# A hybrid attention, recurrence and convolution encoder step: small buffers moved, the last convolution tile's copies on two queues, filler matmuls in the prologue

## The chip, the cores and the metric

The kernel runs on one core of one Trainium2 chip. The metric is device time in microseconds (us), the median of several runs. A core has five engines with a queue each: PE (TensorE, matmuls), DVE (VectorE), ACT (ScalarE), POOL (GpSimd) and SP (SyncE, which here only issues transfers). They run on their own and wait for each other by semaphores. Transfers (DMAs) can be issued from SP, ACT or POOL.

## The reference, cut to what matters

Two layers over 512 prompt frames and 32 frames of a running stream (544 in all), width 1024. Layer 0 has attention and a gated recurrence side by side, layer 1 the convolution module below; each is followed by a feed-forward part.

```python
def conv_module(xn, buf, w1, b1, w_dw, b_dw, ln_g, ln_b, w2, b2):
    u = xn @ w1 + b1
    u = u[..., :D_MODEL] * jax.nn.sigmoid(u[..., D_MODEL:])
    full = jnp.concatenate([buf.astype(u.dtype), u], axis=1)
    y = lax.conv_general_dilated(full, w_dw[:, None, :], window_strides=(1,), padding='VALID',
                                 feature_group_count=D_MODEL) + b_dw      # depthwise, 31 taps
    y = jax.nn.silu(layer_norm(y, ln_g, ln_b))
    return y @ w2 + b2, full[:, -(CONV_W - 1):]

def ffn(xn, w_up, w_down):
    return jnp.square(jax.nn.relu(xn @ w_up)) @ w_down
```

## The kernel before

Activations lie with channels on the 128 partitions, in KT = 8 tiles of 544 frames. A weight matrix is streamed in **units** of 1024 x 256 (1 MB), numbered from 0 over the whole kernel. For accuracy each operand is split into a high and a low part, and every product takes three matmuls. A unit passes through: an SP load into one of two slots of `w_raw` (line 416; the load of unit n waits on `w_lo` until unit n-2 has been split), ACT's copy into `w_h` (`split_hi`, line 608), DVE's difference into `w_l` (`split_lo`, line 1514), and then PE (lines 1017, 1040 and 1056).

`keep_clock(n, bank)` issues n bf16 matmuls of 256 columns on the constant tile `ones` into a PSUM bank that is free. Their results are read by no one.

**Prologue.** SP loads the frames as rows (`x_rows`), PE turns them (line 996), DVE and ACT copy them into `resid` (semaphores `x_copied`, one for each of four PSUM slots; DVE copies tiles 0 to 5 at line 1568, ACT tiles 6 and 7 at line 661), ACT and DVE make `x_h` and `x_l`, and `together(0, 0, ...)` multiplies unit 0 tile by tile (line 1040, 96 matmuls), each tile after its `xl_ready`. `parameters()` (lines 1077 to 1085) and unit 1 (line 1017) follow. The sums of squares of the rows go to `x_ss` and their inverse roots to `x_rs`, two tiles of 128 x 5.

**Convolution.** Units U_PW1 + m, m = 0 to 7, make the two halves of channel tile m. ACT takes the sigmoid (`gate`, line 894), DVE the product (`gated_frames`, line 1912, into `glu`; it raises `slot_free[1]`). PE does 20 or, in the last tile, 24 of the 31 taps as 32 x 32 diagonal matmuls (`taps`, line 1398); for them `glu_rot` holds `glu` rotated by 32, 64 and 96 partitions, which takes six DMAs a tile, issued by POOL (lines 579 and 580, semaphores `moved[m % 2]`, 96 a tile). DVE does the other taps (line 1936) and the stream's frames (lines 1948 to 1952) and adds PE's part (`conv_sum`, line 1961). PE's order at the end is: unit of tile 7, `taps(6)`, `add_mean(0)` to `add_mean(3)` (line 1414), `taps(7)`, `add_mean(4)` to `add_mean(7)`, the variance (line 1438), and the second pointwise matmul, units U_PW2 to U_PW2 + 3.

```python
            for j in range(1, ROTS):
                at = P - j * (P // ROTS)
                pool.dma_start(glu_rot[0:at, m % 2, j - 1, :], glu[P - at:P, m, 0:PAD + SEQ]).then_inc(moved[m % 2], 16)
                pool.dma_start(glu_rot[at:P, m % 2, j - 1, :], glu[0:P - at, m, 0:PAD + SEQ]).then_inc(moved[m % 2], 16)
```

All order is written out by hand; there is no scheduler. The lines in the text below are those of the kernel before.

Of the kernel before, what the change touches and what calls it, by code (L numbers as in the profile page):

```python
# [24 lines left out]
P = 128  # L25
D = 1024
KT = D // P
SEQ, DEC = 512, 32
TOK = SEQ + DEC
HALF = TOK // 2  # L30
TT = SEQ // P
# [8 lines left out]
PAD = CONV - 1  # L40
CW = SEQ + PAD + DEC + 2
ROTS = 4
# [9 lines left out]
U_PW1 = U_FFN0 + 8 * NF  # L52
U_PW2 = U_PW1 + 8
# [21 lines left out]
def tile0(u):  # L75


    return 8 + 2 * u
# [6 lines left out]
def hybrid_kernel(nc, x_prompt, x_sample, cache_a_k, cache_a_v, state_b, cache_c, norm_mix_g, norm_ffn_g,  # L85
# [6 lines left out]
    def sb(stack, name, shape, dt=F32):  # L92
        return stack.enter_context(nc.sbuf_tensor(name, shape, dt))

    def sem(name):
        return ctx.enter_context(nc.semaphore(name))
# [32 lines left out]
    xn = sb(ctx, "xn", [P, 3, TOK])  # L129
    small = sb(ctx, "small", [P, 16])  # L130
    no_use = sb(ctx, "no_use", [P, 1])
    x_ss = sb(ctx, "x_ss", [P, TT + 1])
    x_rs = sb(ctx, "x_rs", [P, TT + 1])


    with ExitStack() as over:
# [13 lines left out]
    with ExitStack() as over:  # L150
        sb(over, "under_x", [P, 2, KT, TOK])
        with ExitStack() as mix:
            x_rows = sb(mix, "x_rows", [P, TT + 1, D])
            dw_rows = sb(mix, "dw_rows", [CONV, D])
            dw_cross = sb(mix, "dw_cross", [CROSS, D])
            cc_rows = sb(mix, "cc_rows", [PAD, D])
            r_wide = sb(mix, "r_wide", [P, TT + 1, P])

        with ExitStack() as mix:
            proj = sb(mix, "proj", [P, N_PROJ, TOK])  # L160
            lr = sb(mix, "lr", [RANK, TOK])
            with ExitStack() as part:
                qk_sq = sb(part, "qk_sq", [P, 8, TOK])
                wlr = sb(part, "wlr", [P, KT, RANK])
                wlr_h = sb(part, "wlr_h", [P, KT, P], F32R)
                wlr_l = sb(part, "wlr_l", [P, KT, P], F32R)
            with ExitStack() as part:
                bias = sb(part, "bias", [P, 4, 512])
                cv_rows = sb(part, "cv_rows", [P, 2, HA * DA])
                probs = sb(part, "probs", [P, 6, 512])  # L170

                mean_row = sb(part, "mean_row", [P, 2 * P])
                pick_row = sb(part, "pick_row", [P, HB, P])
            with ExitStack() as part:

                sb(part, "under_pair", [P, 3072])
                pair = sb(part, "pair", [P, 2, 2, P])

        with ExitStack() as mix:
            glu = sb(mix, "glu", [P, KT, FW])  # L180
            cv = sb(mix, "cv", [P, KT, CW])
            sig = sb(mix, "sig", [P, 2, TOK])

            glu_rot = sb(mix, "glu_rot", [P, 2, ROTS - 1, PAD + SEQ])
            windows = sb(mix, "windows", [P, DEC, CONV])
            diag = sb(mix, "diag", [P, 2, PE_TAPS, P // ROTS])
            fold_2 = sb(mix, "fold_2", [P, P // 2])
            fold = sb(mix, "fold", [P, P // ROTS])  # L190
        y_rows = sb(over, "y_rows", [P, 2, TT + 1, P])
        y_fin = sb(over, "y_fin", [P, 2, TOK])
# [43 lines left out]
    def width(c):  # L236
# [7 lines left out]
    w_hi, w_lo = sem("w_hi"), sem("w_lo")  # L244
    consts, ones_ready = sem("consts"), sem("ones_ready")
    gains_T, gains_ready = sem("gains_T"), sem("gains_ready")
    r_ready, x_sums, r_rows, r_spread, r_T = (
        sem(n) for n in ("r_ready", "x_sums", "r_rows", "r_spread", "r_T"))

# [129 lines left out]
    @block.sync  # L379
    def _(sp):  # L380
        xp = x_prompt[0].rearrange("(c p) d -> c p d", p=P)
        for c in range(TT):
            sp.dma_start(x_rows[:, c, :], xp[c]).then_inc(x_landed[c], 16)
        sp.dma_start(x_rows[0:DEC, TT, :], x_sample[0]).then_inc(x_landed[TT], 16)

        def load_parameters():
            for at, n, src in ((V_B1, 16, as_rows(c_b_pw1)), (V_BDW, 8, as_rows(c_b_dw)), (V_LNG, 8, as_rows(c_ln_g)),
                               (V_LNB, 8, as_rows(c_ln_b)), (V_B2, 8, as_rows(c_b_pw2)), (V_GB, 2, as_rows(b_gate_b)),
                               (V_ON, 1, b_out_norm_g)):
                sp.dma_start(vec_rows[at:at + n, :], src).then_inc(rows_landed, 16)  # L390
            for at, src in ((V_QG, a_q_norm_g), (V_KG, a_k_norm_g)):
                for b in range(2):
                    sp.dma_start(vec_rows[at:at + 1, b * DA:(b + 1) * DA], src).then_inc(rows_landed, 16)
            sp.dma_start(wlr[:], w_view(w_in_ab[0])[:, :, N_PROJ * P:N_PROJ * P + RANK]).then_inc(rows_landed, 16)
            sp.dma_start(dw_rows[:], c_w_dw[0]).then_inc(rows_landed, 16)
            for j in range(1, ROTS):
                to, of = (a.rearrange("t (k h c) -> t k h c", h=ROTS, c=P // ROTS) for a in (
                    dw_cross[(j - 1) * SET:j * SET], c_w_dw[0, j * SET:(j + 1) * SET]))
                sp.dma_start(to[:, :, 0:ROTS - j, :], of[:, :, j:ROTS, :]).then_inc(rows_landed, 16)
                sp.dma_start(to[:, :, ROTS - j:ROTS, :], of[:, :, 0:j, :]).then_inc(rows_landed, 16)  # L400
            sp.dma_start(cc_rows[:], cache_c[0, 0]).then_inc(rows_landed, 16)
            sp.dma_start(gate_w[:], b_gate_w_up[0]).then_inc(rows_landed, 16)
            sp.dma_start(rel, a_rel_bias[0]).then_inc(rows_landed, 16)
            sp.dma_start(state_s[:], state_b[0, 0].rearrange("(a b) k v -> (b k) a v", b=2)).then_inc(rows_landed, 16)

        def stream(u0, units, source, first=False):

            if first:
                for s in range(2):
                    sp.dma_start(w_raw[:, s], source(s)).then_inc(w_landed[s], 16)  # L410
                load_parameters()
            with sp.Fori(1 if first else 0, units // 2) as i:
                for s in range(2):

                    sp.wait_ge(w_lo, i * 2 + (u0 + s - 1))
                    sp.dma_start(w_raw[:, s], source(i * 2 + s)).then_inc(w_landed[s], 16)

        def columns(w, at=0):
            v = w_view(w)
            return lambda n: v[:, :, bass.ds(n * 256 + at, 256)]  # L420

        def ffn(layer, u0):
            for n, (way, c) in enumerate(FFN_ORDER):
                src = (columns(w_ffn_up[layer], c * D) if way == "up"
                       else columns(w_ffn_down[layer][c * D:(c + 1) * D, :]))
                stream(u0 + 4 * n, 4, src)

        stream(U_IN, 12, columns(w_in_ab[0]), first=True)

        sp.wait_ge(pairs_done, 10)  # L430
        stream(U_OUT, 4, columns(w_out_ab[0]))
        ffn(0, U_FFN0)

        stream(U_PW1, 8, columns(c_w_pw1[0]))
        stream(U_PW2, 4, columns(c_w_pw2[0]))
        ffn(1, U_FFN1)

        yp = y_prompt[0].rearrange("(c p) d -> p c d", p=P)
        for k in range(KT):
            sp.wait_ge(y_stage, 2 * (k + 1))  # L440
            sp.dma_start(yp[:, :, k * P:(k + 1) * P], y_rows[:, k % 2, 0:TT, :]).then_inc(y_stored[k % 2], 16)
            sp.dma_start(y_sample[0][:, k * P:(k + 1) * P], y_rows[0:DEC, k % 2, TT, :])\
                .then_inc(y_stored[k % 2], 16)
        for n in range(2):
            sp.wait_ge(y_stored[n], 32 * (KT // 2))
# [3 lines left out]
    def _(pool):  # L449
# [123 lines left out]
        for m in range(KT):  # L573

            pool.wait_ge(slot_free[1], m + (tile0(U_PW1) // 2 + 1))
            pool.wait_ge(taps_done, m + 1)
            for j in range(1, ROTS):
                at = P - j * (P // ROTS)
                pool.dma_start(glu_rot[0:at, m % 2, j - 1, :], glu[P - at:P, m, 0:PAD + SEQ]).then_inc(moved[m % 2], 16)
                pool.dma_start(glu_rot[at:P, m % 2, j - 1, :], glu[0:P - at, m, 0:PAD + SEQ]).then_inc(moved[m % 2], 16)  # L580

        pool.wait_ge(edges_out, 2)
        pool.dma_start(cc_prompt[0, 0], ccn[0]).then_inc(stored, 16)
# [6 lines left out]
    def _(act):  # L590
# [293 lines left out]
                    last(u)  # L884

        ffn(0, U_FFN0, lambda u: phase(u, 4, squares_of(2, u)))
        norm(2, X_MIX1)


# [16 lines left out]

        act.wait_ge(glu_edges, 7)

        split_hi(U_PW1, 0, 1)
        with act.Fori(0, KT // 2 - 1) as i:  # L910
            for s in range(2):
                gate(i, s)
# [7 lines left out]
        gate(KT // 2 - 1, 1)  # L920

        split_hi(U_PW2, 0, 1)
        act.activation(no_use[:], eps[:], ACT.Sqrt)

        def cv_deviation(c):
# [47 lines left out]
    def _(pe):  # L973
# [165 lines left out]
                ins.then_inc(r_T, 1)  # L1139
            pe.wait_ge(xl_ready, X_MIX0 + k + 1)  # L1140

        for n in range(4):
            pe.wait_ge(x_copied[n], 2)
        together(0, 0, x_h, x_l, x_ready)
        parameters()
# [237 lines left out]
        def taps(m):  # L1383
# [1 line left out]
            s = m % 2  # L1385
            pe.wait_ge(diag_ready, m + 1)
            pe.wait_ge(slot_free[1], m + (tile0(U_PW1) // 2 + 1))
            pe.wait_ge(moved[s], (m // 2 + 1) * 96)

            if m:  # L1390
                pe.wait_ge(conv_step, m * STEPS)
# [33 lines left out]
        pe.wait_ge(slot_free[0], tile0(U_PW2) // 2)  # L1425
        for k in range(4):
            add_mean(k)
        taps(KT - 1)
        for k in range(4, KT):
            add_mean(k)  # L1430
# [648 lines left out]
```

## Time and profile before

| what | us |
|---|---|
| median of 3 runs | 1373.24 (1372.77 to 1374.39) |
| the profiled execution's own time | 1374.85 |
| its span, from the first to the last instruction | 1373.1 |
| PE busy in it | 1344.9 (98%) |
| DVE, ACT, POOL busy | 703.2, 472.7, 86.5 |

The profiled execution took 1.75 us more than its span, and 1.61 us more than the median of the runs. Mean granted TensorE clock: 0.993 of full speed. A granted clock of 1.00 is 2.4 GHz and one of 0.50 is 1.2 GHz.

### The profile page before, as it was taken

The page shows a single profiled execution, that of the slowest core. Times are in us where ns is not written, and L with a number is a line of the kernel's source. Part 1 is how long each engine was busy: PE and PEld are TensorE (multiplying, and loading weights), DVE is VectorE, ACT ScalarE, POOL GpSimd, SP SyncE. Part 2 cuts the span into 40 slices and gives each one's busy share as a digit, 9 for nine tenths or more (in the row PEclk, how much of TensorE's full clock was granted, in tenths as well). Part 3 has the DMA queues.
Part 4 walks back from the last instruction along what each step waited for, and adds up shares of the span by engine and source line. Part 5 has one row for each costly group of instructions (what it writes and reads, how often), then busy time and mean ns, then how long its engine had stood idle before and what let it go on. Part 6 is the DMA issues. An engine that isn't in the chain of part 4 may idle for free.

```text
span 1373.1 us, 27650 instructions
## 1 busy us (share of the span) xinstructions
PE 1344.9 (98%) x11649; PEld 1274.7 (93%) x11649; DVE 703.2 (51%) x1028; ACT 472.7 (34%) x792; POOL 86.5 (6%) x145
## 2 busy tenths in 40 slices
PE   8999999999999999999999999989999999999998
PEld 7998888779999999999999888858999999999998
DVE  5693568575544334334324788877544334334322
ACT  4221556434333223123122544445433223223111
POOL 4001100001100000000011111101100000000000
PEclk9999999999999999999999999999999999999999
DMA  7223300222222222222221433302222221222221
GB/s 253 80 92 106 119 27 2 95 72 93 82 83 82 92 92 92 92 85 74 96 84 62 112 110 106 104 16 69 93 93 92 93 92 61 95 90 92 92 78 50
DMA packets 107293, 119.90 MB, mean 87 GB/s; under 512 B 4435, under 2 KB 103358, under 8 KB 106943
## 3 DMA queue, kind: packets, MB, share of 16 engines
q1 hardware_dynamic: 102783, 101.50, 23.1%
q0 software_dynamic: 4352, 17.02, 4.2%
q8 instruction: 72, 1.18, 0.3%
q14 instruction: 22, 0.18, 0.0%
q10 hardware_dynamic: 64, 0.02, 0.0%
HBM read 104.66 MB, written 7.21 MB: 81 GB/s over the span
## 4 chain that ended last, share of the span: by engine, by line
PE 90%; DVE 5%; ACT 2%; issue 2%; DMA 1%; POOL 0%; SPq 0%; DVEq 0%; ACTq 0%; POOLq 0%
PE ps L1017 70%; PE ps L1173 4%; PE ps L1398 3%; PE ps L1040 3%; DVE rstd L1613 2%; PE ps L1190 1%; PE ps L1284 1%; PE ps L980 1%; PE ps L1223 1%; PE ps L1207 1%; PE ps L1056 1%; PE ps L1002 1%; DVE w_l L1514 1%; PE ps L1438 1%; DMA x_rows<-in_x_sample 1%
## 5 line engine op out<-in xcount | busy, mean ns | idle before, releaser
L608 ACT ACTIVATE w_h<-w_raw 128x2048 fp32r<-128x2048 f32 x92 | 175.4, 1907 | 276.4 <-PE ps L1017 272.9
L1514 DVE TENSOR_TENSOR w_l<-w_raw,w_h 128x2048 fp32r<-128x2048 f32 x92 | 210.8, 2291 | 102.8 <-ACT w_h L608 102.7
L1017 PE MATMUL ps<-x_h,w_h 128*128 128x272 f32 x1152 | 242.0, 292 | 2.4 <-ACT sig L894 1.5
L1017 PE MATMUL ps<-x_l,w_h 128*128 128x272 f32 x1152 | 238.6, 288 | 0.0
L1017 PE MATMUL ps<-x_h,w_l 128*128 128x272 f32 x1152 | 238.2, 288 | 0.0
L1017 PE MATMUL ps<-xf_h,w_h 128*128 128x272 f32 x1024 | 212.9, 289 | 0.0
L1017 PE MATMUL ps<-xf_l,w_h 128*128 128x272 f32 x1024 | 211.2, 287 | 0.0
L1017 PE MATMUL ps<-xf_h,w_l 128*128 128x272 f32 x1024 | 210.9, 287 | 0.0
L1017 PEld LDWEIGHTS ps<-x_h,w_h 128*128 128x128 f32 x1152 | 180.9, 189 | 9.1 <-issue 8.7
L1017 PEld LDWEIGHTS ps<-x_l,w_h 128*128 128x128 f32 x1152 | 182.6, 189 | 0.0
L1017 PEld LDWEIGHTS ps<-x_h,w_l 128*128 128x128 f32 x1152 | 180.7, 188 | 0.0
L1017 PEld LDWEIGHTS ps<-xf_l,w_h 128*128 128x128 f32 x1024 | 161.5, 188 | 0.0
L1017 PEld LDWEIGHTS ps<-xf_h,w_h 128*128 128x128 f32 x1024 | 159.9, 188 | 0.2
L1017 PEld LDWEIGHTS ps<-xf_h,w_l 128*128 128x128 f32 x1024 | 159.8, 188 | 0.0
L1861 DVE TENSOR_TENSOR resid<-ps,resid 128x544 f32 x64 | 46.3, 724 | 200.6 <-PE ps L1017 199.7
L870 ACT ACTIVATE relu<-relu 128x544 f32<-128x544 f32 x64 | 42.2, 659 | 239.9 <-DVE relu L1879 239.9
L1017 PE MATMUL ps<-odd_h,w_h 128*128 128x272 f32 x512 | 106.8, 290 | 0.0
L1017 PE MATMUL ps<-odd_l,w_h 128*128 128x272 f32 x512 | 105.6, 287 | 0.0
L1017 PE MATMUL ps<-odd_h,w_l 128*128 128x272 f32 x512 | 105.5, 287 | 0.0
L1879 DVE SCALAR_TENSOR_TENSOR relu<-ps,xn 128x544 f32<-128x544 f32 x64 | 46.2, 722 | 89.6 <-PE ps L1017 89.5
L1017 PEld LDWEIGHTS ps<-odd_l,w_h 128*128 128x128 f32 x512 | 80.8, 188 | 0.0
L1017 PEld LDWEIGHTS ps<-odd_h,w_l 128*128 128x128 f32 x512 | 79.9, 188 | 0.0
(278 smaller groups left out, 1653.5 us busy)
## 6 DMA issues: line engine op xcount, KB each, us to landing
w_raw<-in_w_ffn_up SPq DMA_DIRECT2D x32, 1024.0 KB, 5.3
w_raw<-in_w_ffn_down SPq DMA_DIRECT2D x32, 1024.0 KB, 5.1
w_raw<-in_w_in_ab SPq DMA_DIRECT2D x12, 1024.0 KB, 5.3
w_raw<-in_c_w_pw SPq DMA_DIRECT2D x12, 1024.0 KB, 6.1
w_raw<-in_w_out_ab SPq DMA_DIRECT2D x4, 1024.0 KB, 5.5
glu_rot<-glu POOLq DMA_DIRECT2D x16, 203.2 KB, 5.4
resid_scratch<-resid POOLq DMA_DIRECT2D x1, 2176.0 KB, 8.1
resid<-resid_scratch POOLq DMA_DIRECT2D x1, 2176.0 KB, 9.0
```

The source lines that it names most:

```text
L608: act.activation(w_h[s][:], w_raw[:, s], ACT.Copy).then_inc(w_hi, 1)
L870: act.activation(relu2[:, m, :], relu[:, m, :], ACT.Square).then_inc(relu2_done, 1)
L980: pe.matmul(ps[:, bank, 0:2 * P], any_bits[:, 0:P], any_bits, start=True, stop=True)
L1002: ins = pe.matmul(dst[:, a, :], w[:], src[:, a * n:(a + 1) * n], start=start, stop=stop)
L1017: ins = pe.matmul(ps[:, 2 * m + t, 0:HALF], a[s][:, k, w], b[:, k, t * HALF:(t + 1) * HALF], start=(k == 0 and q == 0), stop=(k == KT - 1 ...
L1040: ins = pe.matmul(ps[:, 2 * m + t, 0:HALF], a[s][:, k, w], b[:, k, t * HALF:(t + 1) * HALF], start=(k == 0 and q == 0), stop=(k == KT - 1 ...
L1173: ins = pe.matmul(ps[:, 2 * m + t, 0:HALF], a[u % 2][:, k, m * P:(m + 1) * P], b[:, k, t * HALF:(t + 1) * HALF], start=(k == 0 and q == 0) ...
L1398: ins = pe.matmul(ps[to, 4 + r, :], diag[rows, s, tap, :], src, start=(n == 0), stop=(n == rounds(m) - 1))
L1514: dve.tensor_tensor(w_l[s][:], w_raw[:, s], w_h[s][:].bitcast(F32), ALU.subtract).then_inc(w_lo, 1)
L1613: dve.reciprocal(rstd[:, 0:TOK], sumsq[:]).then_inc(rstd_ready, 1)
L1861: dve.tensor_tensor(r, slot(m), r, ALU.add).then_inc(slot_free[m], 1)
L1879: dve.scalar_tensor_tensor(out=halves(relu[:, m, :]), in0=slot(m), scalar=0.0, in1=halves(r_tok), op0=ALU.max, op1=ALU.mult).then_inc(slot ...
```

## The change

Six edits:
- `x_ss` and `x_rs` are allocated behind `r_wide` in the region that later stages reuse, no longer in front of `x_h`; what follows them starts a little lower in memory.
- Tile 7's second copy of each rotation (32, 64 and 96 partitions) is issued by ACT, behind `split_hi` of unit U_PW2 + 1, on a semaphore `moved_last`; POOL issues only the other three.
- SP waits for all six of those copies before it loads units U_PW2 + 2 and U_PW2 + 3.
- `split_hi` of unit U_PW1 + 1 stands before the third norm on ACT, no longer behind it.
- Twenty filler matmuls stand between the turning of the rows and unit 0.
- Eight filler matmuls stand in front of `taps(7)`.

```diff
-    x_ss = sb(ctx, "x_ss", [P, TT + 1])
-    x_rs = sb(ctx, "x_rs", [P, TT + 1])
...
             r_wide = sb(mix, "r_wide", [P, TT + 1, P])
+            x_ss = sb(mix, "x_ss", [P, TT + 1])
+            x_rs = sb(mix, "x_rs", [P, TT + 1])
...
-        stream(U_PW2, 4, columns(c_w_pw2[0]))
+        stream(U_PW2, 2, columns(c_w_pw2[0]))
+
+        sp.wait_ge(moved[(KT - 1) % 2], KT // 2 * 96 - 48)
+        sp.wait_ge(moved_last, 48)
+        stream(U_PW2 + 2, 2, columns(c_w_pw2[0], 512))
...
-                pool.dma_start(glu_rot[at:P, m % 2, j - 1, :], glu[0:P - at, m, 0:PAD + SEQ]).then_inc(moved[m % 2], 16)
+                if m < KT - 1:
+                    pool.dma_start(glu_rot[at:P, m % 2, j - 1, :], glu[0:P - at, m, 0:PAD + SEQ])\
+                        .then_inc(moved[m % 2], 16)
...
         ffn(0, U_FFN0, lambda u: phase(u, 4, squares_of(2, u)))
+        split_hi(U_PW1, 0, 1)
         norm(2, X_MIX1)
...
         act.wait_ge(glu_edges, 7)
 
-        split_hi(U_PW1, 0, 1)
...
         split_hi(U_PW2, 0, 1)
+
+        act.wait_ge(slot_free[1], KT - 1 + (tile0(U_PW1) // 2 + 1))
+        act.wait_ge(taps_done, KT)
+        for j in range(1, ROTS):
+            at = P - j * (P // ROTS)
+            act.dma_start(glu_rot[at:P, (KT - 1) % 2, j - 1, :], glu[0:P - at, KT - 1, 0:PAD + SEQ])\
+                .then_inc(moved_last, 16)
         act.activation(no_use[:], eps[:], ACT.Sqrt)
...
-        for n in range(4):
+        for n in range(2):
+            pe.wait_ge(x_copied[n], 2)
+        keep_clock(20, 0)
+        for n in range(2, 4):
             pe.wait_ge(x_copied[n], 2)
         together(0, 0, x_h, x_l, x_ready)
...
-            pe.wait_ge(moved[s], (m // 2 + 1) * 96)
+            if m < KT - 1:
+                pe.wait_ge(moved[s], (m // 2 + 1) * 96)
+            else:
+                pe.wait_ge(moved[s], (m // 2 + 1) * 96 - 48)
+                pe.wait_ge(moved_last, 48)
...
         for k in range(4):
             add_mean(k)
+        pe.wait_ge(slot_free[1], tile0(U_PW2) // 2)
+        keep_clock(8, 2)
         taps(KT - 1)
```

How the order moves at three places. First PE in the prologue, between the last turned rows and unit 0. Before:

```order
L996 MATMUL ps<-ident,x_rows 128x128 [waits x_copied3]
L996 MATMUL ps<-ident,x_rows 128x128 x3
L996 MATMUL ps<-ident,x_rows 128x32
L1040 MATMUL ps<-x_h,w_h 128x272 [waits w_lo,slot_free0,x_copied3,slot_free1,x_copied2,xl_ready,x_copied1,x_copied0]
L1040 MATMUL ps<-x_h,w_h 128x272
```

And now (the lines are those of the changed kernel):

```order
L1010 MATMUL ps<-ident,x_rows 128x128 [waits x_copied3]
L1010 MATMUL ps<-ident,x_rows 128x128 x3
L1010 MATMUL ps<-ident,x_rows 128x32
L994 MATMUL ps<-ones 128x256 [waits x_copied1,x_copied0]
L994 MATMUL ps<-ones 128x256 x19
L1054 MATMUL ps<-x_h,w_h 128x272 [waits slot_free0,slot_free1,w_lo,xl_ready,x_copied3,x_copied2]
L1054 MATMUL ps<-x_h,w_h 128x272
```

Twenty fillers have come in front of unit 0; they wait only for the copies of PSUM slots 0 and 1.

Second, PE in front of `taps(7)`. Before:

```order
L1414 MATMUL ps<-cv,mean_d 128x288 [waits conv_ready]
L1414 MATMUL ps<-cv,mean_d 128x288
L1398 MATMUL ps<-glu,diag 32x512 [waits moved1,conv_step,slot_free1,diag_ready]
L1398 MATMUL ps<-glu,diag 32x512 x3
L1398 MATMUL ps<-glu_rot,diag 32x512 x12
```

And now:

```order
L1435 MATMUL ps<-cv,mean_d 128x288 [waits conv_ready]
L1435 MATMUL ps<-cv,mean_d 128x288
L994 MATMUL ps<-ones 128x256 [waits slot_free1]
L994 MATMUL ps<-ones 128x256 x7
L1419 MATMUL ps<-glu,diag 32x512 [waits moved_last,moved1,conv_step,slot_free1,diag_ready]
L1419 MATMUL ps<-glu,diag 32x512 x3
L1419 MATMUL ps<-glu_rot,diag 32x512 x12
```

Eight fillers have come in front of the taps, and the taps wait for two semaphores of copies, no longer for one.

Third, ACT at the end of the convolution tiles. Before:

```order
L894 ACTIVATE sig<-ps,vecs 128x544 [waits gemm_done]
L608 ACTIVATE w_h<-w_raw 128x2048 [waits gemm_done,w_landed1]
L923 ACT_TABLE_LOAD
L923 ACTIVATE no_use<-eps 128x1
L934 ACTIVATE sq<-cv 128x288 [waits cv_centred] x4
```

And now:

```order
L902 ACTIVATE sig<-ps,vecs 128x544 [waits gemm_done]
L615 ACTIVATE w_h<-w_raw 128x2048 [waits gemm_done,w_landed1]
L935 DMA glu_rot<-glu 32x542 [waits taps_done,slot_free1]
L935 DMA glu_rot<-glu 64x542
L935 DMA glu_rot<-glu 96x542
L937 ACT_TABLE_LOAD
L937 ACTIVATE no_use<-eps 128x1
L948 ACTIVATE sq<-cv 128x288 [waits cv_centred] x4
```

ACT now issues three DMAs, of 32, 64 and 96 partitions, between its weight copy and a table load.

## Rows read from the trace of the kernel before

**Rows 1.** The page, parts 1 and 4: PE's load, the chain's shares

```profile
PE 1344.9 (98%) x11649; PEld 1274.7 (93%) x11649; DVE 703.2 (51%) x1028; ACT 472.7 (34%) x792; POOL 86.5 (6%) x145
PE 90%; DVE 5%; ACT 2%; issue 2%; DMA 1%; POOL 0%; SPq 0%; DVEq 0%; ACTq 0%; POOLq 0%
```

**Rows 2.** Windows of the prologue: stretch, length, five engines, granted clock, DMA share, GB/s

```profile
19.00:20.00 1.00, 1.00 (x6) 1.00 (x5) 1.00 (x2) 1.00 (x3) 0.00 (x0) 0.50 0.18 51
...
22.00:23.00 1.00, 1.00 (x11) 1.00 (x10) 0.00 (x0) 0.97 (x3) 0.00 (x0) 1.00 0.30 88
```

**Rows 3.** Timeline of PE in the prologue: start, us, instructions, idle before and releaser

```profile
10.40 5.56 PE L996 MATMUL ps<-ident,x_rows 32*128 32x32 f32 x36 [0.26 <-DMA x_rows<-in_x_sample]
18.25 0.61 PE L1040 MATMUL ps<-x_h,w_h 128*128 128x272 f32 x2 [2.28 <-DVE x_l L1536]
...
21.83 0.44 PE L1040 MATMUL ps<-x_h,w_l 128*128 128x272 f32 x2
22.11 0.42 PE L1040 MATMUL ps<-x_h,w_h 128*128 128x272 f32 x2
22.36 0.41 PE L1040 MATMUL ps<-x_l,w_h 128*128 128x272 f32 x2
```

**Rows 4.** Timeline of DVE in the prologue

```profile
13.72 1.49 DVE L1568 COPY resid<-ps 128x544 f32<-128x544 f32 x2
...
17.32 4.26 DVE L1536 SCALAR_TENSOR_TENSOR x_l<-resid,vecs,x_h 128x544 fp32r<-128x544 f32 x6
```

**Rows 5.** The chain that ended last, behind unit 0

```profile
32.90 0.07 PE ps L1077
...
34.58 12.28 PE ps L1017 x96
```

**Rows 6.** Timeline of PE: 28 fillers on end in front of the third norm

```profile
740.09 3.23 PE L980 MATMUL ps<-ones 128*128 128x256 bf16 x28
```

**Rows 7.** Timeline of SP, DVE and POOL at tile 7, of ACT's early DMA

```profile
886.91 0.37 SPq L416 DMA_DIRECT2D w_raw<-in_c_w_pw  x1
...
886.66 1.03 DVE L1912 SCALAR_TENSOR_TENSOR glu<-ps,vecs,sig 128x272 f32<-128x272 f32 x3
...
887.98 0.52 POOL L579 DMA_DIRECT2D glu_rot<-glu  x1 [14.62 <-DVE glu L1912]
...
1.27 0.44 ACTq L599 DMA_DIRECT2D vec_rows<-in_norm_ffn_g  x1
```

**Rows 8.** Timeline of PE, then the chain that ended last, at tiles 6 and 7

```profile
889.22 4.15 PE L1414 MATMUL ps<-cv,mean_d 128*128 128x288 f32 x16
...
866.14 5.47 PE ps L1398 x148
...
890.51 6.70 DMA glu_rot<-glu
...
897.45 8.87 PE ps L1398 x186
```

**Rows 9.** Windows in front of and in `taps(7)`, columns as in rows 2

```profile
895.00:896.00 1.00, 0.00 (x0) 0.00 (x0) 1.00 (x3) 0.00 (x0) 0.00 (x0) 0.83 0.08 26
...
902.00:903.00 1.00, 1.00 (x38) 0.39 (x10) 0.00 (x0) 0.00 (x0) 0.00 (x0) 0.75 0.00 0
```

**Rows 10.** DMAs from 860 to 915 us: KB each, median us to landing

```profile
glu_rot<-glu POOLq DMA_DIRECT2D x4, 67.8 KB, 5.2
```

**Rows 11.** Timeline of DVE: its last work for tile 7 before `conv_sum`

```profile
899.07 0.24 DVE L1952 TENSOR_SCALAR cv<-cv,vecs 128x32 f32<-128x32 f32 x1
```

**Rows 12.** Timeline of ACT at the third norm, of PE at tile 1

```profile
744.68 0.71 ACT L643 ACTIVATE sumsq<-ps,eps 128x544 f32<-128x544 f32 x1 [2.69 <-PE ps L1002]
...
765.27 0.49 PE L1017 MATMUL ps<-x_h,w_h 128*128 128x272 f32 x2 [1.52 <-ACT sig L894]
```

**Rows 13.** Timeline of ACT: its copy of unit U_PW2 + 2

```profile
943.68 1.90 ACT L608 ACTIVATE w_h<-w_raw 128x2048 fp32r<-128x2048 f32 x1
```

**Rows 14.** A window of the attention's start, columns as in rows 2

```profile
140.00:150.00 10.00, 9.12 (x58) 8.92 (x57) 2.98 (x4) 5.65 (x7) 1.13 (x3) 0.76 0.56 197
```

More of the change, by code:

```diff
@@ L246, in hybrid_kernel @@
     gains_T, gains_ready = sem("gains_T"), sem("gains_ready")
+    moved_last = sem("moved_last")
     r_ready, x_sums, r_rows, r_spread, r_T = (
```

## The prediction

> **What bounds the kernel now.** I read the page first, then the chain that ended last, then the timelines and windows of the two places where the chain leaves PE at its full clock, and last the DMA view of the convolution. PE is busy 98% of the span and holds 90% of the chain [rows 1]. So only three things can shorten this kernel: less work on PE, less time in which PE waits, and less time in which it runs at 1.2 GHz. The change takes no work from PE (it adds 28 fillers). What it can give is found in two places.
>
> In the prologue PE ends turning the rows at 15.96 (10.40 + 5.56) and starts unit 0 at 18.25, after 2.28 us idle [rows 3]. Just after that pause the granted clock is 0.50, and it is back at 1.00 by 22 [rows 2]. At the end of the convolution tiles PE ends `add_mean(3)` at 893.37 (889.22 + 4.15), and `taps(7)` starts at 897.45, 0.25 us after the last copy of `glu_rot` lands at 897.21 (890.51 + 6.70) [rows 8]. The clock drops while PE stands idle (0.83 in 895 to 896) and is only coming back in 902 to 903, where the mean is 0.75 [rows 9]. So the taps take 8.87 us [rows 8].
>
> **The small buffers.** The two moves change addresses and nothing else: no instruction, wait or DMA comes or goes. Every operand of unit 0 is read at many starts already (eight tiles, two halves), and PE's matmuls follow each other by the same 0.25 us a pair [rows 3]. I take 0; I see no row that would give either sign.
>
> **Twenty fillers in the prologue.** They wait for PSUM slots 0 and 1 to be copied, which DVE has done at 15.21 (13.72 + 1.49) [rows 4], before PE is through with the rows. So they start at about 15.96. 28 fillers on end took 3.23 us, 0.115 each [rows 6], and 20 take 2.3: they end at 18.26, against 18.25 for unit 0 now. I charge them 0.05. Unit 0 then begins at 1.00. From 18.25 to 21.83 PE issued 8 pairs [rows 3]; at the spacing of 0.25 that follows they take 2.0 and not 3.58. That is 1.58 less, 1.5 after the charge. `x_l` does not hold PE back: its tiles come every 0.71 us from 17.32 on (six in 4.26) [rows 4], and PE wants one in 12 matmuls, 1.5 us. Behind unit 0 the chain runs straight on over the parameters (32.90) and unit 1 (34.58) [rows 5], each released by PE or by what PE released, so the 1.5 us travel to the end. The bounds: nothing, if the parameters' DMAs land only just before 32.90 (the trace shows PE not waiting for them, not how early they are), or if the clock drops all the same; 1.6, if the fillers cost nothing. I take **1.5**.
>
> **The copies of tile 7.** `glu` is ready at 887.69 (886.66 + 1.03), and POOL starts its six DMAs at 887.98, 0.5 us each [rows 7]; the last, issued at 890.51, lands 6.70 us later [rows 8]. In the two tiles from 860 to 915 the usual figure is 5.2 [rows 10]. Now POOL issues three, the last at about 889.0. ACT has finished its weight copy by then, waits for the same `glu`, and issues its three from about 887.8 at 0.44 each [rows 7], the last at about 888.7. With 5.2 to landing, that is 894.2 and 893.9. SP's load of 1 MB, issued at 886.91, 1.07 us ahead of the copies [rows 7], is now held until they have landed. No row shows such copies without a load beside them. So 5.2 may be too much for them, but less would bring nothing: PE's eight new fillers end at 893.37 + 0.9, about 894.3. The taps start at the later of 894.3 and 894.2 + 0.25. I take 894.4 in place of 897.45, so **3.05** (bounds: 3.15 if the fillers decide; 1.5 if the landing takes 6.70 again, 889.0 + 6.70 + 0.25 = 895.95).
>
> The Trainium skill, page "Trainium Kernel Development and Optimization", section Key Constraints, speaks against the half of this that is about queues: DMAs from SP, ACT and POOL share the same 16 engines and interleave, so that issuing from several queues saves only issue time. By it the two queues bring the 1.5 us of POOL's three DMAs, and what is more must come from the held load. Its result is the first rival below.
>
> **The clock in the taps.** With fillers up to 894.3 and taps from 894.4, the pause of 4.08 us that preceded the drop is gone. At full clock the 20 taps of an earlier tile took 5.47 us [rows 8]; the 24 of tile 7 take 6/5 of it, 6.56. That is 8.87 - 6.56 = **2.3** less. Below: 0 if the clock drops anyway. The taps then end at about 901.0, after DVE's last work for the tile at 899.31 (899.07 + 0.24) [rows 11], so `conv_sum` follows PE as it did before, and so does all behind it.
>
> **The held load.** Unit U_PW2 + 2 is loaded from about 894.4 and not from 886.9. ACT wants it at 943.68 [rows 13], more than 40 us later. Behind it on SP's queue stands only U_PW2 + 3, which waits for a later split anyway. Cost 0; with that cover gone it would be the 7.5 us of the delay. ACT's table load behind the three DMAs moves from 885.9 to about 889.2; ACT's next real work is after `conv_sum`. Cost 0.
>
> **The moved `split_hi`.** ACT idles 2.69 us in front of the third norm's root [rows 12], and the copy takes 1.90 [rows 13], on data that are there. It hides, with 0.8 us to spare; without that pause it would cost 1.9. Nor does it gain: PE's start on tile 1 at 765.27 waits for the sigmoid [rows 12], not for this split. 0.
>
> **Sum.** 1.5 + 3.05 + 2.3 = 6.85, say 6.9. The span of the profiled execution goes from 1373.1 to 1366.2, its own time from 1374.85 to about 1368.0. The median of the runs was 1373.24, 1.61 under that execution's; I subtract from the median: **1366.3**. About 0.2% (2.7 us) is what a measurement can tell from no change.
>
> **Rivals.**
> - *Two queues save issue time only, and the held load nothing* (0.12). The copies land 1.5 us sooner, at 895.7, and the taps start at 895.95, after an idle 1.65 us. The clock stays up, since in both places above it was down only after more than 2 us of idleness. Saved: 1.5 + 1.5 + 2.3 = 5.3, so 1367.9. For it: 6.70 at tile 7 shows that a landing can be later than 5.2. Against it: that landing had 1 MB beside it.
> - *The same, and the clock drops again* (0.07). Saved: 1.5 + 1.5 = 3.0, so 1370.2.
> - *The prologue gives nothing* (0.08): the parameters are late, or the clock drops. Saved 5.35: 1367.9.
> - *Low stretches elsewhere come or go* (0.07). Everything behind 20 us runs 1.5 us sooner, and behind 900 us 6.9. Other stretches at 1.2 GHz may change with it: in 140 to 150 the mean of 0.76 costs 2.4 us [rows 14]. It may go, 1363.9, or a like one may be added, 1368.7; the first is as likely as the second.
> - *Slower: ACT's three copies land late* (0.02). No row shows ACT's queue moving data from SBUF to SBUF. If the last lands L us after its issue at 888.7, the taps at the low clock end at 888.7 + L + 0.25 + 8.87 = 897.8 + L, against 906.32 before. With the prologue's 1.5 the balance is a loss only from L = 10.0, and one of over 2.7 from L = 12.7; at L = 15 the kernel takes 1378.2. The nearest figure is 6.70 for the copies of POOL.
> - *Nearly nothing happens* (0.04): the second rival and the third together, 1371.7.
>
> The forecast itself has the remaining 0.60, with a range of its own of 1365.3 to 1367.3.
>
> **How the numbers follow.** The range for 8 in 10 takes in the first, third and fourth rival and reaches to the edge of the second: 1363.6 to 1370.0. Faster by over 0.2% (below 1370.5): the forecast, the first four rivals, 0.94, which I lower to 0.93. Within 0.2%: 0.05. Slower: 0.02.
>
> **What the profile after would show.** PE without a pause between the rows and unit 0, and a clock of 1.00 from 18 to 22; line 1054's first pairs 0.25 apart. The last copies landing near 894, taps of tile 7 starting at 892.9 (894.4 less the prologue's 1.5) and lasting 6.6. SP's load issued just behind the landing. ACT's root of the third norm no later relative to PE. The prediction is wrong if the ACT copies land later than POOL's, if the clock is at 0.50 anywhere in these two places, or if the lead of 1.5 us at unit 1 has been lost by 150 us.

## The result, and the profile after

| | us |
|---|---|
| kernel before, 4 runs | 1373.74 (1372.77 to 1374.39) |
| changed kernel, 4 runs | **1357.27** (1356.06 to 1357.93) |
| ratio, 95% interval | 0.988 (0.9863 to 0.9897) |
| forecast | 1366.3 (1363.6 to 1370.0) |

The kernel became 16.5 us faster, where 6.9 was forecast, and the time lies below the range. The profiled execution after took 1356.06, with a span of 1354.3. The one before had 1373.1, so the profiles differ by 18.8. In both, PE is busy 98% [rows 1].

First the chain that ended last in the changed kernel (start, us, what), with the rows that answer to [rows 5, 8]:

```profile
16.32 2.29 PE ps L994 x20
18.61 9.25 PE ps L1054 x72
33.39 12.17 PE ps L1031 x96
...
135.21 2.07 PE ps L1016 x8
137.28 6.18 PE ps L1031 x48
...
355.23 370.36 PE ps L1031 x2976
...
874.26 5.45 PE ps L1419 x149
879.71 4.08 PE ps L1435 x16
883.79 0.87 PE ps L994 x8
884.66 6.52 PE ps L1419 x179
...
969.22 340.48 PE ps L1031 x2736
```

The same view of the kernel before, where the new rows have their partners (line 1017 has become 1031):

```profile
136.78 2.86 PE ps L1002 x8
139.65 8.54 PE ps L1017 x48
...
360.57 373.67 PE ps L1017 x2976
...
984.74 343.53 PE ps L1017 x2736
```

And windows of the changed kernel (stretch, length, five engines, granted clock, DMA share, GB/s), for [rows 2, 9, 14]:

```profile
18.00:20.00 2.00, 2.00 (x17) 1.72 (x16) 2.00 (x4) 2.00 (x4) 0.00 (x0) 1.00 0.14 40
20.00:22.00 2.00, 2.00 (x18) 2.00 (x18) 1.94 (x3) 2.00 (x4) 0.00 (x0) 1.00 0.53 148
138.00:140.00 2.00, 2.00 (x18) 2.00 (x18) 0.78 (x1) 1.96 (x4) 0.32 (x1) 1.00 1.07 344
884.00:888.00 4.00, 4.00 (x120) 2.30 (x128) 4.00 (x6) 0.00 (x0) 0.00 (x0) 1.00 0.64 212
888.00:892.00 4.00, 4.00 (x98) 2.35 (x85) 2.45 (x5) 0.00 (x0) 0.00 (x0) 1.00 0.16 55
```

What the reader is to see:
- **Prologue.** The fillers stand where they should, the clock is 1.00, and unit 1 starts at 33.39 instead of 34.58: 1.2 less, although the turning of the rows began 0.36 later (timeline: 10.76, against 10.40 in [rows 3]).
- **The pace of PE.** 2976 matmuls took 370.36 instead of 373.67, and 2736 took 340.48 instead of 343.53. Over these groups PE is busy all the time at a granted clock of 1.00 in both kernels (windows of their exact length). It is the same work, 0.9% faster.
- **The stretch at 138.** The 48 matmuls that took 8.54 took 6.18, and the 8 in front of them 2.07 instead of 2.86: 3.15 less together. The windows 138 to 140 and 140 to 150 have clock 1.00, where [rows 14] had a mean of 0.76 over 140 to 150.
- **Tile 7.** From the start of the four `add_mean` to the end of the taps it is 11.54 us (879.64 by the timeline, to 891.18), against 17.10 in [rows 8] (889.22 to 906.32): 5.56 less, forecast 5.35. No DMA is in the chain here any more.

The prologue, the stretch at 138 and tile 7 give 1.2 + 3.15 + 5.56 = 9.9 of the profiles' difference of 18.8. The remaining 8.9 lies in the pace: 6.4 in the two long groups, the rest nearly all in the shorter groups of 272-column matmuls (one of 336 takes 42.05 instead of 42.43, which is 0.9% again). I had set that part to 0. (The expectations below reckon it at 9.6, because they left the 8 matmuls at 136.78 in it. The stretch at 138 belongs to the profile that was caught, as will be seen, and hardly to the medians: there, 8.9 + 5.6 + 1.2 = 15.7 of the 16.5 are accounted for, and the rest is within the spread of the runs.)

### The profile page after: what moved, and what is told of

Its sections match the earlier page's. It is cut to its first block, busy times and chain, and to the rows that moved or that the text cites. A ratio compares the mean times of both kernels' runs of the same rounds, so it can differ in the third digit from the quotient of the medians.

```text
span 1354.3 us, 27697 instructions
## 1 busy us (share of the span) xinstructions
PE 1332.9 (98%) x11677; PEld 1263.7 (93%) x11677; DVE 703.1 (52%) x1028; ACT 472.5 (35%) x792; POOL 84.6 (6%) x142
## 4 chain that ended last, share of the span: by engine, by line
PE 92%; DVE 4%; ACT 2%; issue 1%; DMA 0%; POOL 0%; ACTq 0%; DVEq 0%; POOLq 0%
PE ps L1031 71%; PE ps L1190 4%; PE ps L1419 3%; PE ps L1054 3%; DVE rstd L1636 2%; PE ps L994 2%; PE ps L1207 1%; PE ps L1301 1%; PE ps L1240 1%; PE ps L1224 1%; PE ps L1070 1%; PE ps L1016 1%; DVE w_l L1537 1%; PE ps L1461 1%; PE ps L1010 0%
```

## The experiments

**Theory 1**: the start address of `x_h` and of what lies behind it sets the pace of the matmuls. The move shifted them down by 64 bytes (`x_ss` and `x_rs` took 32 each); the weights `w_h`, `w_l` stayed. **Theory 2**, the rival: the pace came from the other edits, or by the execution.

### The move alone, all but the move, and the same place modulo 256

`e1_move_only` is the kernel before with the move; `e2_all_but_move` the changed kernel with `x_ss`, `x_rs` back; `e3_before_pad192` the kernel before with

```diff
     x_rs = sb(ctx, "x_rs", [P, TT + 1])
+    sb(ctx, "pad", [P, 48])
```

> The kernel before, with x_ss and x_rs moved behind the frames' buffers and nothing else. The buffers behind x_rs (x_h, x_l, xf, odd) start 64 bytes lower, as in the changed kernel. Theory 1 (the start address of the convolutions' and products' operands sets the pace of the 272-column matmuls): the group of 2976 matmuls takes 370.4 instead of 373.7, that of 2736 takes 340.5 instead of 343.5, and the time is 1373.7 - 9.6 = 1364.1. Theory 2 (the pace came from the other edits or from the run): both groups stay at 373.7 and 343.5, and the time stays at 1373.7.

> The changed kernel, with x_ss and x_rs back in their old place: the fillers, the copies by two queues and the moved split_hi alone. Theory 1: the two long groups of matmuls are back at 373.7 and 343.5, and the time is 1357.3 + 9.6 = 1366.9, which is near the 1366.3 of the forecast. Theory 2: they stay at 370.4 and 340.5, and the time at 1357.3.

> The kernel before, with an unused buffer of 192 bytes behind x_rs, so that x_h and all behind it start 192 bytes higher. That is the same place modulo 256 bytes as in the changed kernel, where they start 64 bytes lower. If theory 1 holds with a period of 256 bytes: the long groups take 370.4 and 340.5, the time is 1364.1. If only the lower address or the small buffers' new place helps (or theory 2): 373.7, 343.5 and 1373.7.

The last two columns are the durations of the two long groups, in us:

| kernel | median, runs | ratio to before (95%) | x2976 | x2736 |
|---|---|---|---|---|
| e1_move_only | 1364.54, 6 | 0.9935 (0.9911 to 0.9959) | 370.36 | 340.48 |
| e2_all_but_move | 1367.82, 12 | 0.9972 (0.9953 to 0.999) | 373.67 | 343.53 |
| e3_before_pad192 | 1364.64, 7 | 0.994 (0.9918 to 0.9963) | 370.36 | 340.48 |

The kernel before took 1373.1 beside them. The chain of `e1_move_only`:

```profile
358.51 370.36 PE ps L1017 x2976
978.10 340.48 PE ps L1017 x2736
```

The chain of `e2_all_but_move`:

```profile
356.74 373.67 PE ps L1031 x2976
975.38 343.53 PE ps L1031 x2736
```

Theory 2 falls: the two rows follow the move to a hundredth of a microsecond, with the other edits or without, and they do so in every profile taken (twelve have 370.36 to 370.38 and 340.48 to 340.50 at the distance of the changed kernel). By the medians the move alone gives 8.6 us, and all the other edits together 5.3 (by the interval, 1.4 to 6.5), where 6.9 was forecast for them. The executions of `e2` lie far apart, 1365.43 to 1373.58, at mean granted clocks of 0.999 down to 0.993. `e3` moved nothing but the frames, up by 192 bytes instead of down by 64, and has the fast rows. So it needs neither the lower address nor the small buffers' new home; a place that is the same modulo 256 bytes is enough.

### Which distance

Six further places of `x_h`, by unused bytes ahead of it in the changed kernel (first diff: `m_pad32`, 8 elements of 4 bytes; the others have 96, 128, 160, 192 or 224 bytes), and one of the weights (second diff: `m_w64`, `w_h`, `w_l` and all behind them 64 bytes higher):

```diff
     no_use = sb(ctx, "no_use", [P, 1])
+    sb(ctx, "pad", [P, 8])
```
```diff
+    sb(ctx, "pad", [P, 16])
     with ExitStack() as over:
         w_h, w_l = [], []
```

> The changed kernel with 64 unused bytes ahead of w_h: the weights and all behind them move up by 64, so that the weights stand at 192 modulo 256 (128 in every kernel so far) and x_h at 160, which was its place before the change; their distance is that of the changed kernel. If the place of the moving operand by itself sets the pace: the group of 2976 takes 373.7. If its distance to the weights does: 370.4. A third value would say that both places count.

> The changed kernel with 32 unused bytes ahead of x_h, which then stands at 128 modulo 256, a multiple of 64 (96 in the changed kernel and 160 in the one before are not). If the pace has just two values by which half of the 256 bytes x_h starts in, it is one of 370.4 and 373.7 here. If what counts is how many pieces of 64 bytes a row of 1088 bytes touches (17 from a multiple of 64, 18 from elsewhere), the group is shorter than 370.4.

> The changed kernel with 96 unused bytes ahead of x_h, which then stands at 192 modulo 256, a multiple of 64. Under pieces of 64 bytes: as in m_pad32, below 370.4. Under a dependence on 256 bytes: another value than in m_pad32, since 64 bytes made the difference between 370.4 and 373.7.

> The changed kernel with 160 unused bytes ahead of x_h, which then stands at 0 modulo 256. Under pieces of 64 bytes: below 370.4, as m_pad32 and m_pad96. Its rows start at 0, 64, 128 and 192 as theirs do, in another order of halves and k, so a difference among the three comes from which start goes with which weights, not from the starts by themselves.

> The changed kernel with 224 unused bytes ahead of x_h: x_h at 64 modulo 256, 64 below the weights' place (distance -64). If a distance and its mirror gave one pace, it would be that of +64 (370.37 in the group of 2976); but +32 and -32 already differ. If negative distances are the good ones: 370.4 or less in both long groups. If all multiples of 64 but +64 are alike: 372.84 and 342.75.

> The changed kernel with 128 unused bytes ahead of x_h: distance +96 modulo 256. Positive distances that are no multiple of 64 slow (as +32): 373.7 and 343.5. If the pace repeats every 128 bytes, +96 is -32: 370.4 and 340.5.

> The changed kernel with 192 unused bytes ahead of x_h: distance -96 modulo 256. If negative distances are the good ones: 370.4 and 340.5. If the pace repeats every 128 bytes, -96 is +32: 373.7 and 343.5.

> The kernel of m_pad96 once more. If the two long groups' different paces (370.37 and 343.52) belong to their places in the program: the same two values. If the pace is one of two that an execution falls into: another pair, such as 373.7 and 343.5 or 370.4 and 340.5.

One execution each, and their times go the same way: 1358.47 for `m_w64`, 1366.9 for `m_pad192`. Distance is the start of `x_h` less that of `w_h`, modulo 256; the column beside it is the same modulo 128:

| kernel | x_h, w_h (mod 256) | distance | mod 128 | x2976 | x2736 |
|---|---|---|---|---|---|
| before, e2_all_but_move | 160, 128 | +32 | 32 | 373.67 | 343.53 |
| m_pad192 | 32, 128 | -96 | 32 | 373.68 | 343.54 |
| changed, e1, e3 | 96, 128 | -32 | 96 | 370.36 | 340.48 |
| m_w64 | 160, 192 | -32 | 96 | 370.36 | 340.48 |
| m_pad128 | 224, 128 | +96 | 96 | 370.38 | 340.50 |
| m_pad32 | 128, 128 | 0 | 0 | 372.84 | 342.75 |
| m_pad160 | 0, 128 | +128 | 0 | 372.84 | 342.75 |
| m_pad96 | 192, 128 | +64 | 64 | 370.37 | 343.52 |
| m_pad96_again | 192, 128 | +64 | 64 | 373.66 | 343.52 |
| m_pad224 | 64, 128 | -64 | 64 | 370.36 | 342.01 |

The chain of `m_w64`, the sharpest case:

```profile
357.35 370.36 PE ps L1032 x2976
...
971.35 340.48 PE ps L1032 x2736
```

`x_h` stands where it stood before the change, in the slow place, and the rows are the fast ones, since the weights have moved too. So it is not the place of the moving operand but its distance to the weights, and at distances of 32, 96 and 0 modulo 128 the pace repeats every 128 bytes. Two guesses of the expectations fell on the way: "negative distances are the good ones" with `m_pad128` and `m_pad192`, and the pieces of 64 bytes with `m_pad32`. A row of `x_h` is 2176 bytes, 128 modulo 256, so a shift of 128 only swaps even and odd channel tiles, which fits the period; that is an argument, not a run. At a distance of 64 modulo 128 the pace isn't fixed: one kernel gave 370.37 and 373.66 in two executions, and `m_pad224` took 342.01 in its second group, between the fast and the slow value. So nothing is said of a period there.

The chain of `m_pad96`, then that of the same kernel once more:

```profile
356.03 370.37 PE ps L1032 x2976
...
970.59 343.52 PE ps L1032 x2736
```

```profile
354.44 373.66 PE ps L1032 x2976
...
972.35 343.52 PE ps L1032 x2736
```

### The end of the convolution, one part at a time

`e4_no_hold` gives SP back its four loads in a row; `e5_one_queue` lets POOL issue all six copies; `e8_one_queue_no_hold` does both; `e6_no_8` leaves the eight fillers out.

```diff
-        stream(U_PW2, 2, columns(c_w_pw2[0]))
-
-        sp.wait_ge(moved[(KT - 1) % 2], KT // 2 * 96 - 48)
-        sp.wait_ge(moved_last, 48)
-        stream(U_PW2 + 2, 2, columns(c_w_pw2[0], 512))
+        stream(U_PW2, 4, columns(c_w_pw2[0]))
```
```diff
-                if m < KT - 1:
-                    pool.dma_start(glu_rot[at:P, m % 2, j - 1, :], glu[0:P - at, m, 0:PAD + SEQ])\
-                        .then_inc(moved[m % 2], 16)
+                pool.dma_start(glu_rot[at:P, m % 2, j - 1, :], glu[0:P - at, m, 0:PAD + SEQ])\
+                    .then_inc(moved[m % 2] if m < KT - 1 else moved_last, 16)
```
```diff
-        pe.wait_ge(slot_free[1], tile0(U_PW2) // 2)
-        keep_clock(8, 2)
         taps(KT - 1)
```

> The changed kernel without the held weight load: SyncE issues the load of the product's weights in the order of before, ahead of the last tile's copies' end. If sharing between this load and the copies matters: the copies land later than 5.8 after issue, tile 7's taps start later than 884.7, and the time rises above 1357.3 by up to the 5 of that load. If not (the forecast of 0 for the hold): taps start at 884.7, 1357.3.

> The changed kernel with all six copies of tile 7 issued by GpSimd, as before the change, and the weight load still held. Without the hold (run e4) the taps of tile 7 start 8.9 after glu's last piece is there, with hold and two queues 6.3. If the hold is what lands the copies sooner and the second queue adds its issue time only: the last copy is issued about 1.2 later than with two queues and lands 4 to 5 after it, so the taps start 7.3 to 7.7 after glu, and the time is about 1 above the changed kernel, 1358.5. If the second queue is needed for the gain: taps start 9 or more after glu, and the time is 1360.

> The changed kernel with six copies by GpSimd and the weight load not held: of the change at this place only the 8 products that fill the wait are left. Copies and load run side by side as in the kernel before, so the taps of tile 7 start 9.75 after glu there. Against run e4 (two queues, not held, 8.9) this tells what the second queue gives by itself: 0.9, if its use is the issue time alone. Expected time: 1357.3 + 3.4 = 1360.7.

> The changed kernel without the 8 products that fill the wait ahead of tile 7's taps. If they are what keeps the clock in the taps: the clock drops within them as before, the group of 179 matmuls takes up to 8.9 instead of 6.5, and the time is 1357.3 + 2.3 = 1359.6, less the part of the fillers that ran past the copies' landing (at most 0.9). If the shorter wait alone keeps the clock: 6.5 stays and the time is 1357.3 - 0.4 = 1356.9 or the same.

The third column is from the start of `glu`'s last piece to the start of `taps(7)`, which doesn't depend on how early the kernel came there (before: 886.66 to 897.45 [rows 7, 8]):

| kernel | median | glu to taps | taps |
|---|---|---|---|
| before | - | 10.79 | 8.87 |
| e8: one queue, no hold | 1362.24 | 10.11 | 7.91 |
| e4: two queues, no hold | 1359.65 | 9.91 | 6.58 |
| e5: one queue, hold | 1359.72 | 7.49 | 6.53 |
| changed: two queues, hold | 1357.27 | 7.49 | 6.52 |
| e6: changed without the 8 | 1358.29 | 6.83 | 6.58 |

The medians are from different chips, with 1373.1 (e4), 1372.44 (e5, e6, e8) and 1373.74 beside them; the ratios are 0.9908 (0.9883 to 0.9934), 0.9906 (0.9884 to 0.9929), 0.9896 (0.9875 to 0.9917) and 0.9921 (0.9901 to 0.9941) for e4, e5, e6, e8, and overlap, so I go by the profiles. DMA view of the changed kernel (KB each, median us to landing), which answers to [rows 10]:

```profile
w_raw<-in_c_w_pw SPq DMA_DIRECT2D x1, 1024.0 KB, 5.1
glu_rot<-glu POOLq DMA_DIRECT2D x1, 203.2 KB, 3.1
glu_rot<-glu ACTq DMA_DIRECT2D x1, 203.2 KB, 4.7
...
glu_rot<-glu POOLq DMA_DIRECT2D x1, 67.8 KB, 4.2
```

The same view of `e4_no_hold`:

```profile
w_raw<-in_c_w_pw SPq DMA_DIRECT2D x1, 1024.0 KB, 5.7
glu_rot<-glu POOLq DMA_DIRECT2D x1, 203.2 KB, 5.3
glu_rot<-glu ACTq DMA_DIRECT2D x1, 203.2 KB, 7.3
...
glu_rot<-glu POOLq DMA_DIRECT2D x1, 67.8 KB, 6.9
```

And of `e5_one_queue`:

```profile
glu_rot<-glu POOLq DMA_DIRECT2D x2, 203.2 KB, 3.0
glu_rot<-glu POOLq DMA_DIRECT2D x2, 135.5 KB, 3.0
glu_rot<-glu POOLq DMA_DIRECT2D x2, 67.8 KB, 3.0
```

The hold is what makes the copies land sooner: without it, PE waits for a copy that takes 7.3 instead of 4.7. Over all profiles, glu to taps is 6.83 to 7.63 in the fifteen with the hold and 9.28 to 10.79 in the five without it. What the second queue gives without the hold can't be told. `e8` and `e4` differ by 0.2, but the four profiles with one queue and no hold spread from 9.28 (`e3_before_pad192`) over 10.11 (`e8`) and 10.41 (`e1_move_only`) to 10.79 (before), and the 9.91 of `e4` lies among them. With the hold nothing shows either. Six copies from one queue land 3.0 after their issue, three from each of two up to 4.7 after it, so that the last one lands 6.9 after the start of `glu`'s last piece in `e5` and 7.0 in the changed kernel: what was saved in issuing is given back in landing. In both of these kernels the fillers, not the copies, decide the start of the taps.

The Trainium skill, "Trainium Kernel Development and Optimization", section Key Constraints, has the rule that the queues share the same 16 engines, so that more queues save issue time at most. The traces agree (6.9 and 7.0).

The clock: PE's pause ahead of `taps(7)` by the timelines of `e4_no_hold`, then of `e8_one_queue_no_hold`:

```profile
883.80 1.04 PE L990 MATMUL ps<-ones 128*128 128x256 bf16 x8
887.26 0.63 PE L1415 MATMUL ps<-glu,diag 32*32 32x512 f32 x4 [2.43 <-DMA glu_rot<-glu]
```

```profile
886.35 1.04 PE L982 MATMUL ps<-ones 128*128 128x256 bf16 x8
890.01 1.07 PE L1407 MATMUL ps<-glu,diag 32*32 32x512 f32 x4 [2.62 <-DVE cv L1947]
```

(The second row of `e8` names DVE, line 1947. But of DVE's steps the taps of tile 7 need only those of tile 6, which ended at 884.96. The last copy, issued at 883.75 and landed some 6.0 later, is what PE waited for.)

2.43 us of idleness cost nothing in the taps (6.58, with a granted clock of 1.00 throughout), 2.62 us cost 1.4 (7.91, with 0.50 in the window 890 to 892), the 2.67 of `e3_before_pad192` cost 1.65, the 3.81 of `e1_move_only` 2.6 and the 4.08 of before 2.35. So the cost does not simply grow with the pause, and the two cases of 2.43 and 2.62 are one profile each. With the hold, the short wait keeps the clock, and the eight fillers aren't needed for it: without them PE paused 0.21 (`e6_no_8`) and 0.82 (`b1_no_8_again`), and the taps took 6.58 both times. In the changed kernel they end 0.46 us behind the last copy's landing (issued at 879.5, 4.7 to landing: 884.2, against 884.66). In `e6_no_8` that landing took 4.2 and the taps began 0.66 sooner relative to `glu`.

### Without the twenty

> The changed kernel without the 20 products in the prologue. The forecast's term: unit 0 starts at the lower clock, its matmuls' end and with it unit 1 is 1.5 later: 1357.3 + 1.5 = 1358.8. A second possibility: the three kernels profiled so far without these 20 products (the kernel before, e1, e3) have a stretch at 1.2 GHz around 138 to 146, and the three with them (the changed kernel, e2, e4) have none. If the 20 products are its cause, it is back here, and the time is 1357.3 + 1.5 + 2.4 = 1361.2. If it comes and goes by itself, 1358.8 in most executions.

`e7_no_20` drops `keep_clock(20, 0)`. It took 1360.03 (ratio 0.9906, 0.9885 to 0.9928). From the first of the chain's turned rows to unit 1 it is 24.00 us (10.20 to 34.20), with unit 0's first 72 matmuls in 10.63; in the changed kernel 22.56 (10.83 to 33.39), with 9.25. So the twenty give 1.4. All other profiles bear this out: the same stretch takes 22.53 to 22.68 in fourteen of the sixteen with the twenty, and 24.00 to 24.18 in three of the four without them. In the other three (`b1_no_8_again`, `m_pad128` and, without the twenty, `e3_before_pad192`) it takes 26.7 to 26.9, with the clock at 0.50 while the rows are turned. The chain of `e7_no_20` at the second place that this run was to judge:

```profile
138.84 8.55 PE ps L1031 x48
```

The low stretch is back here, but `e5_one_queue` has it too, with the twenty products (8.14), and `e6_no_8` as well (7.75). The idea that the twenty always take it away falls; whether they make it rarer is open.

### A version without the eight, beside the changed kernel

> The changed kernel without the 8 products ahead of tile 7's taps, timed beside the changed kernel itself. By the profiles, from the start of tile 6's taps to the end, it is 0.6 shorter (474.90 against 475.50). If that is a gain of the kernel: a median 0.6 below b2_after_again. If the clock is lost in the taps in other executions: at or above it.

> The changed kernel once more, on the chip of b1_no_8_again. 1357.3 if this chip is like the first; the stretch at the lower clock around 138 to 146, which its first profile does not have, may be there, and makes the time up to 3 longer.

| kernel | median, 6 runs | ratio to before (95%) |
|---|---|---|
| b1_no_8_again | 1359.57 (1355.82 to 1361.59) | 0.9902 (0.9881 to 0.9924) |
| b2_after_again | 1356.56 (1354.98 to 1361.84) | 0.9899 (0.9874 to 0.9923) |

The two overlap widely, and the clock sorts them more than the edit does: `b2` took 1354.98 at a mean granted clock of 0.999 and 1361.77 at 0.994, `b1` 1355.82 at 0.999 and 1361.59 at 0.994. This pair also measures the change once more, with six runs against eleven: 15.9 us by the medians (1372.41 to 1356.56). Without the eight no gain shows. In the profile of `b1_no_8_again` the last copy of ACT landed 4.8 after its issue, and `glu` to taps is 7.44, as with the fillers: the 0.66 of `e6_no_8` was the luck of one landing. The chain of `b1_no_8_again` in the prologue:

```profile
10.09 8.20 PE ps L1010 x36
18.29 4.14 PE ps L994 x20
36.96 12.17 PE ps L1031 x96
...
140.86 7.73 PE ps L1031 x48
```

and a window of it:

```profile
18.00:22.00 4.00, 4.00 (x20) 2.84 (x20) 4.00 (x6) 3.59 (x6) 0.00 (x0) 0.50 0.31 93
```

The twenty fillers were there and PE was never idle from 11 us on, and still the clock stood at 1.2 GHz from 12 to 22: the turned rows took 8.20 instead of 5.50, the fillers 4.14 instead of 2.29, and unit 1 started 3.6 later than in the changed kernel's profile. The chain of `b2_after_again`, the very program of the changed kernel, has `136.57 7.75` where its first profile had 6.18. So the stretch at 138 comes and goes by the execution (five of the twenty profiles are without it: the changed kernel, `e2`, `e4` and both of `m_pad96`), and it can't be booked to the change.

## Why the prediction was wrong

- **"The small buffers. I take 0; I see no row that would give either sign."** This is the step that failed. It was worth 8.9 of the 18.8 us between the profiles, and 8.6 by the medians of `e1`. It argued that the operands are read at many starts already, so that a shift can't matter. But the starts aren't random: rows are 2176 bytes and halves 1088, so all reads fall on four starts modulo 256, and their pairing with the weights repeats exactly in each tile of 48 matmuls. The move changed that pairing everywhere. `e1` gives it alone, `e2` takes it away, and `m_w64` shows that the distance counts and not the place. "Changes addresses and nothing else" was true, and addresses were worth more than all the rest (5.3 by `e2`). It should have stood as an unknown with bounds of both signs. What it would be worth could have been bounded: PE is at such matmuls for most of the 1373 us, and 1% of their pace is about 10 us.
- **Twenty fillers, 1.5.** Right: 1.4 by `e7` against the changed kernel, 1.3 to 1.65 over the profiles in which the clock held. They ended when they should (18.61 with rows that came 0.36 later), and the lead was not lost later. Their bound "if the clock drops all the same" does occur (`b1`, `m_pad128`).
- **The copies, 3.05.** The size held (glu to taps fell from 10.79 to 7.49, by 3.3), the split not. The forecast gave 1.5 to POOL's shorter issuing, and 1.55 to a landing of 5.2 instead of 6.70 with the load held. Shown is the hold with 2.4 (9.91 to 7.49, `e4` against the changed kernel) and the queue with nothing that can be told. That the two sums agree is in part luck. ACT issued at 0.61 each, not the 0.44 of [rows 7], and the copies' last landing was 4.7, not 5.2; both errors were small and hidden by the fillers, which decided the start, as the forecast's other bound (3.15) had it.
- **The clock in the taps, 2.3.** Right in size: 6.52 where 6.56 was worked out, 2.35 less than 8.87. Its cause is the shorter wait, not the eight fillers (`e6`, `b1`).
- **The held load, 0 for its delay.** Right: it was issued at 884.40, at once behind the copies, and nothing behind it waited.
- **The moved `split_hi`, 0.** As forecast. By ACT's timeline after, the copy took 733.20 to 735.09, the norm's root still found 0.89 idle ahead of it, and PE's start on tile 1 still followed the sigmoid.
- **The rivals.** "Two queues save issue time only" had its first half right (less than issue time, even), but its second, "the held load nothing", was wrong by about 2, so its 1367.9 missed as well. "Low stretches come or go" happened between the two profiles (3.15), and can't be seen in the medians. No case had the pace of PE in it, and that is why the range was too narrow: it covered mishaps of the steps that I had costed, not an error in the one that I had set to nothing.

What stays open: why a distance of 96 modulo 128 is the fast one, and why 64 has several values. The runs show the map, not the cause. A pairing of reads in memory between the moving operand and the load of the next weights would fit it (PEld is busy all through the long groups, as PE is), but no run separates the two reads, nor either of them from what ACT and DVE write into `w_h` and `w_l` beside the matmuls.

## What to carry to other kernels

When PE is at 98%, an edit that only moves buffers is not free of effect: compare the long groups of matmuls in the chain, whose duration repeats to 0.02 us, before explaining a time by waits, and try a few pads between the stationary and the moving operand. Where small copies on the critical path meet a large load that is not urgent, hold the load; for a second queue no gain could be told here. And a low stretch of the clock in one profile is booked to a change only after the same program has been profiled twice.

## What the runs showed of the hardware

- In this kernel the pace of the 128 x 272 matmuls of the split operands depends on the distance between the moving operand's and the weights' start, modulo 128 bytes: 370.36 us at 96, 372.84 at 0 and 373.67 at 32 for the same 2976 matmuls, the same in each kernel of a class to 0.02.
- At a distance of 64 modulo 128 one program falls into different paces in different executions (370.37 and 373.66 for the 2976, `m_pad96`), and 2736 matmuls can take a time between the fast and the slow one (342.01, `m_pad224`).
- The granted clock can be at 1.2 GHz in the prologue while PE is never idle (`b1_no_8_again`, 0.50 in 18 to 22), and at 2.4 GHz in the same place in the same program at other times (e6_no_8: unit 1 at 32.54, against 36.96).
- A pause of PE of 2.43 us left the granted clock at 1.00 (`e4`); after pauses of 2.62 and 2.67 us it was down (`e8`: 0.50 in 890 to 892; `e3`: a mean of 0.57 in 892 to 896).
- Six copies from SBUF to SBUF by one queue landed in 3.0 each (`e5`), and three by each of two queues in 2.6 to 4.8. Beside a load of 1 MB they took 4.8 to 6.7 by one queue and 5.3 to 7.3 by two.
